# Retention's output products in high and low parts, and 32 pairs of convolution taps multiplied on ScalarE

## The chip, the core and the metric

One Trainium2 chip, one of its cores. The metric is the device time of one execution of the whole program, in microseconds. Engines are named as in the profile: PE is TensorE, with PEld its weight loads, DVE is VectorE, ACT is ScalarE, POOL is GpSimd, SP is SyncE, which issues the loads.

## What is computed

Two blocks over 256 tokens of width 1024, in fp32. The first (gated delta rule, short convolution) is not touched by the change. The second one projects the normalized input into nine pieces and runs two branches over them:

```python
q, k, v, z_ret, u_val, u_gate, z_conv, g_a, g_b = jnp.split(h @ w_in[l], split_at, axis=-1)
# retention: 4 heads, keys of 256, values of 512
scores = einsum('bhid,bhjd->bhij', qc, kc) * decay_mask
inner  = einsum('bhij,bhje->bhie', scores, vc)            # the output products
y_a = (head_groupnorm(o) * silu(z_ret)) @ w_ret_out
# convolution: causal, one filter of 31 taps for each of the 1024 channels
a = u_val * sigmoid(u_gate)
a = causal_depthwise_conv_2(a, conv_w, conv_b)
y_b = (silu(layernorm(a)) * silu(z_conv)) @ w_conv_out
y = (sigmoid(g_a) * y_a + sigmoid(g_b) * y_b) @ w_out
```

The kernel computes the retention without the chunked recurrence: the masked, decayed scores of 256 x 256 tokens times the values.

## The kernel before

**Phases and chunks.** The weights come in chunks of 1 MB, one after the other (`PHASES`, with the number of chunks of each). In the second block the order is glu (8), qk (8), v (8), zret (8), zconv (4), gates (8), ret_out (8), conv_out (4), w_out (4). TensorE goes through the chunks in that order; work that belongs to no chunk stands behind a chunk (`beside`).

**Every product in three.** A weight half chunk (128 x 1024 fp32) is split: ScalarE writes the high part `w_hi` (a copy into the reduced type fp32r, L1220), VectorE the low part `w_lo` = weight minus high part (`part_lo`, L1786). TensorE multiplies high by high, high by low and low by high (in `wide_hi`, L727 and L728, and `wide_lo`, L734, with 512 columns; in `chunk`, L677, L678 and L686, with 256). A wide chunk is 24 products of 128x512. Within a half TensorE waits for `hi_ready` first and for `lo_ready` two thirds on. `w_hi` and `w_lo` have four half slots, so the high part of half h of chunk c can be written when TensorE has done half h of chunk c-2 (`half_done`).

**The step of the other engines.** ScalarE and VectorE run, in program order, one step for each chunk c (`chunks`): first the parts of half 1 of chunk c+1 and of half 0 of chunk c+2, then what the phase gives them (`each`). VectorE's part of it in each phase:

- `rotate` (qk): three operations of the convolution, then the rotation of a 128x512 result out of PSUM (L2445 to L2449).
- `decayed` (v): nine operations of the convolution in steps 0 to 3, eight in 4 to 7, and in steps 0 to 3 the masked scores of a head, `st` (L2459). The values are copied out of PSUM by ScalarE (`tokens_out`, L1641) after every second chunk.
- `group_norm` (zret): seven operations of the convolution, the statistics of one output product (L2477), and in even steps the scalars of the head before (`group_scale`).
- `turned_pairs` (zconv): eight, five, five, five operations, and two low parts of the retention's output, `yT_lo`.
- `last_pairs` (gates): four, then ten in each step until none is left; then the sum over the channels, on which the layer norm of ret_out rests.

**The convolution.** Channels lie in eight groups of 128 partitions, `aP` holds them with 30 zeros in front, `cv` the sums. One operation (`conv_op`, L2396 for tap 0, L2399 for the others) is one tap of one group, 256 wide: `cv = aP[tap:tap+256] * w + cv`. Two groups, a pair, alternate, so that an operation waits on `cv_step` not for the one in front of it but for the one before that. 248 operations in all, in the order pair, tap, group, handed out by `conv_share(n)`.

**The retention.** TensorE computes the scores of head c behind chunk c of v (`scores`, L1134) as fp32 products. Behind chunk c of zret it computes one output product of head c/2 and token block c%2 (`weighted_sums`): one fp32 product of 128x128 by 128x512 for block 0 (L1146), two for block 1 (L1146 and L1148). The profile shows each fp32 product as two instructions. The result lies in one of four PSUM banks. ScalarE normalizes a head's two results in `group_norm` (L1656 square root, L1662), two steps later, and GpSimd multiplies them by the gate (L1773) into `vt`. GpSimd also adds up `cv` of pairs 0 and 1 and then pair 2 (L1777, L1780), when the products by the gate are done and the pair is finished. In zconv TensorE transposes the result (`turn_two`), ScalarE and VectorE write its high and low parts.

**Banks.** In v, zret and gates chunks c and c+1 fill two banks, and chunk c+4 waits until they are read (`bank_free`). Where the reader changes from VectorE to ScalarE or back (`READ_BY`, `HANDED`), the new reader first waits for the old one's last release.

## Time and profile before

| | us |
|---|---|
| three runs | 837.55, 837.8, 839.03 |
| median | 837.8 |
| profiled execution, its own time | 837.87 |
| its span | 836.1 |
| TensorE busy | 827.8 (99%) |
| VectorE busy | 731.1 (87%) |
| ScalarE busy | 500.2 (60%) |
| GpSimd busy | 45.4 (5%) |

The granted TensorE clock is 0.999 of full speed over the span. In the profiled execution the chunks of qk begin at 521.5 us, those of v at 567.6, those of zret at 616.6, of zconv at about 670.8, of gates at 697.2 and of ret_out at about 741. A busy share is the union of an engine's instructions; an instruction can begin before the one in front of it on the same engine has ended, so a duration is longer than the distance between two starts.

### The profile page before, as it was taken

How to read it: one execution, taken by the hardware profiler on the slowest of the kernel's cores; microseconds unless marked ns; L12 is line 12 of the kernel's file. 1: busy time of each engine (PE TensorE's matmuls, PEld its weight loads, DVE VectorE, ACT ScalarE, POOL GpSimd, SP SyncE). 2: the span in 40 equal slices, each digit the busy share in tenths (PEclk: the TensorE clock that was granted, in tenths of full speed). 3: DMA queues.
4: the chain of work that ended last, by engine and by line, in shares of the span. 5: the costliest groups of instructions: out<-in, count | busy, mean ns of one | idle time of the engine just before them, and what ended most of it. 6: DMA issues, size and time to landing. Idle time of an engine off the chain costs nothing.

```text
span 836.1 us, 13942 instructions
## 1 busy us (share of the span) xinstructions
PE 827.8 (99%) x5146; PEld 725.1 (87%) x5146; DVE 731.1 (87%) x1179; ACT 500.2 (60%) x804; POOL 45.4 (5%) x46
## 2 busy tenths in 40 slices
PE   8999999999999999999999999999999999999997
PEld 8999998789888888888888788998887798888886
DVE  7799899868877898888989979999999999988774
ACT  6899858576566555555565775333346675546743
POOL 0001101341100000000000000000001220000000
PEclk9999999999999999999999999999999999999999
DMA  9875675511875877777776656655454435564531
GB/s 277 256 253 169 211 245 174 146 38 45 278 232 179 261 262 263 257 256 252 238 257 218 221 185 213 202 184 169 155 198 151 152 118 200 186 231 171 188 115 50
DMA packets 129882, 164.13 MB, mean 196 GB/s; under 512 B 17407, under 2 KB 92199, under 8 KB 129703
## 3 DMA queue, kind: packets, MB, share of 16 engines
q1 hardware_dynamic: 129831, 163.45, 59.9%
q8 instruction: 33, 0.54, 0.3%
q14 instruction: 18, 0.15, 0.1%
HBM read 159.20 MB, written 4.23 MB: 195 GB/s over the span
## 4 chain that ended last, share of the span: by engine, by line
PE 98%; DVE 1%; DMA 1%; issue 0%; ACT 0%; DVEq 0%; SPq 0%; ACTq 0%
PE psum L695 16%; PE psum L727 14%; PE psum L728 14%; PE psum L734 14%; PE psum L704 8%; PE psum L677 6%; PE psum L686 6%; PE psum L678 6%; PE psum L1028 2%; PE psum L631 1%; PE psum L641 1%; PE psum L635 1%; PE psum L1033 1%; PE psum L915 1%; PE psum L1146 1%; PE psum L1134 1%
## 5 line engine op out<-in xcount | busy, mean ns | idle before, releaser
L1220 ACT ACTIVATE w_hi<-w_raw 128x1024 fp32r<-128x1024 f32 x255 | 266.6, 1061 | 188.2 <-PE psum L734 87.1
L1786 DVE TENSOR_TENSOR w_lo<-w_raw,w_hi 128x1024 fp32r<-128x1024 f32 x256 | 305.2, 1221 | 44.3 <-ACT w_hi L1220 42.2
L695 PE MATMUL psum<-hT,w_hi 128*128 128x512 f32 x576 | 138.9, 391 | 0.0
L695 PEld LDWEIGHTS psum<-hT,w_hi 128*128 128x128 f32 x576 | 105.4, 188 | 20.2
L727 PE MATMUL psum<-w_hi,hT 128*128 128x512 f32 x280 | 113.3, 405 | 0.0
L728 PE MATMUL psum<-w_hi,hT 128*128 128x512 f32 x280 | 109.3, 390 | 0.0
L2399 DVE SCALAR_TENSOR_TENSOR cv<-aP,par,cv 128x256 f32<-128x256 f32 x240 | 107.9, 519 | 0.0
L677 PE MATMUL psum<-hT,w_hi 128*128 128x256 f32 x432 | 107.4, 286 | 0.0
L678 PE MATMUL psum<-hT,w_hi 128*128 128x256 f32 x432 | 105.9, 283 | 0.0
L677 PEld LDWEIGHTS psum<-hT,w_hi 128*128 128x128 f32 x432 | 82.8, 192 | 0.4 <-issue 0.2
L678 PEld LDWEIGHTS psum<-hT,w_hi 128*128 128x128 f32 x432 | 82.9, 192 | 0.3 <-issue 0.2
L704 PEld LDWEIGHTS psum<-hT,w_lo 128*128 128x128 f32 x576 | 74.8, 191 | 3.3
L704 PE MATMUL psum<-hT,w_lo 128*128 128x256 f32 x576 | 76.1, 283 | 0.0
L727 PE MATMUL psum<-w_hi,yT_hi 128*128 128x512 f32 x192 | 75.8, 395 | 0.0
L734 PE MATMUL psum<-w_lo,hT 128*128 128x512 f32 x280 | 75.6, 390 | 0.0
L728 PE MATMUL psum<-w_hi,yT_lo 128*128 128x512 f32 x192 | 74.8, 390 | 0.0
L727 PEld LDWEIGHTS psum<-w_hi,hT 128*128 128x128 f32 x280 | 52.6, 188 | 12.0 <-issue 1.7
L728 PEld LDWEIGHTS psum<-w_hi,hT 128*128 128x128 f32 x280 | 52.6, 188 | 12.0 <-issue 1.7
L734 PEld LDWEIGHTS psum<-w_lo,hT 128*128 128x128 f32 x280 | 52.6, 188 | 11.2
L686 PE MATMUL psum<-hT,w_lo 128*128 128x256 f32 x432 | 60.6, 283 | 0.0
L686 PEld LDWEIGHTS psum<-hT,w_lo 128*128 128x128 f32 x432 | 55.7, 192 | 0.0
L734 PE MATMUL psum<-w_lo,yT_hi 128*128 128x512 f32 x192 | 52.7, 389 | 0.0
(341 smaller groups left out, 1108.6 us busy)
## 6 DMA issues: line engine op xcount, KB each, us to landing
w_raw<-in_w_in_dram SPq DMA_DIRECT2D x44, 1024.0 KB, 5.1
w_raw<-in_sc_w_in_dram SPq DMA_DIRECT2D x32, 1024.0 KB, 7.9
w_raw<-in_gdn_w_in_dram SPq DMA_DIRECT2D x23, 1024.0 KB, 7.1
ada<-in_w_ada_dram SPq DMA_DIRECT2D x24, 512.0 KB, 4.8
w_raw<-in_gdn_w_out_dram SPq DMA_DIRECT2D x8, 1024.0 KB, 5.5
w_raw<-in_sc_w_out_dram SPq DMA_DIRECT2D x8, 1024.0 KB, 6.4
w_raw<-in_w_ret_out_dram SPq DMA_DIRECT2D x8, 1024.0 KB, 5.1
w_raw<-in_w_conv_out_dram SPq DMA_DIRECT2D x4, 1024.0 KB, 5.1
```

The lines of the kernel that those rows point to most:

```text
L677: pe.matmul(o[:, m, :], w_hi[s][:, k, mine], a_hi[:, ka, :], start=m == 0 and ka == 0, stop=False, skip_group_check=True)
L678: pe.matmul(o[:, m, :], w_hi[s][:, k, mine], a_lo[:, ka, :], start=False, stop=False, skip_group_check=True)
L686: mm = pe.matmul(o[:, m, :], w_lo[s][:, k, mine], a_hi[:, ka, :], start=False, stop=ka == KT - 1, skip_group_check=True)
L695: pe.matmul(o, w_hi[s][:, k, mine], hT[:, h * KH2 + k, :, :], start=h == 0 and k == 0, stop=False, skip_group_check=True)
L704: mm = pe.matmul(o, w_lo[s][:, k, mine], hT_hi[:, ka, :], start=False, stop=ka == KT - 1, skip_group_check=True)
L727: pe.matmul(psum[:, b + m, :], a_hi[:, ka, mine], wide(w_hi[s])[:, e, :], start=start and h == 0 and e == 0, stop=False, skip_group_check= ...
L728: pe.matmul(psum[:, b + m, :], a_lo[:, ka, mine], wide(w_hi[s])[:, e, :], start=False, stop=False, skip_group_check=True)
L734: mm = pe.matmul(psum[:, b + m, :], a_hi[:, k + 2 * h + e, mine], wide(w_lo[s])[:, e, :], start=False, stop=stop and h == 1 and e == 1, sk ...
L1028: mm = pe.matmul(b[:, a, :], left(a), right(a), start=True, stop=True)
L1220: act.activation((w_hi[half_slot(g, h)] if home is None else third_hi[half_slot(g, home)])[:, :, :], raw[slot][:, h * KH2:(h + 1) * KH2, : ...
L1786: return dve.tensor_tensor(o, whole, hi.bitcast(F32), ALU.subtract)
L2399: dve.scalar_tensor_tensor(out=cv[:, n, :], in0=src, scalar=w, in1=cv[:, n, :], op0=ALU.mult, op1=ALU.add).then_inc(cv_step, 1)
```

## The change

It has two parts.

*Output products.* The masked scores `st` and the values get high and low parts: ScalarE writes `st_hi` and `vt_hi` (the latter in place of the copy of the values), VectorE `st_lo` and `vt_lo`, in the steps of v. `weighted_sums` multiplies in three, 3 products for block 0 and 6 for block 1 instead of 1 and 2 fp32 ones. The values' banks are now released by VectorE, so the reader changes at zret rather than at v.

*Convolution.* The order of the operations is laid out at build time. 32 (pair, tap) entries are "made": ScalarE multiplies both groups of the pair by their weight (two 256-wide activations) into one of two, later two other, buffers, and VectorE adds the 512-wide buffer to `cv` in one operation. The list `CONV` has 184 single operations and 32 made ones, 216 in all. Per step, singles and made: qk 3 and 0, 3 and 1 in turn; v 6 and 1 four times, 4 and 2 four times; zret 4 and 2 (in step 0: 6 and 2, where a pair ends); zconv 8, 5, 5, 5; gates 4, 10, 10, 10, 7, and none from step 5 on, where the kernel before has 4, five times 10, and 1.

```diff
-READ_BY = {name: "act" if name in ("z", "v", "zret", "zconv", "gates") else "dve" for name in ORDER}
+READ_BY = {name: "act" if name in ("z", "zret", "zconv", "gates") else "dve" for name in ORDER}
+CONV_SHARES = [("glu", [(0, 0), (0, 0), (3, 0), (4, 0), (5, 0), (4, 0), (2, 0), (4, 0)]), ("qk", [(3, 0), (3, 1)] * 4), ("v", [(6, 1)] * 4 + [(4, 2)] * 4),
+               ("zret", [(4, 2)] * 8), ("zconv", [(8, 0), (5, 0), (5, 0), (5, 0)]), ("gates", [(4, 0)] + [(10, 0)] * 7)]
+def tap_before(i):
+    kind, pair, tap, e = CONV[i]
+    return max(j for j in range(i) if CONV[j][1] == pair and (e is None or CONV[j][3] in (None, e))) + 1
...
             def weighted_sums(c):
-                pe.wait_ge(st_ready, min(RH, c + 1))
+                pe.wait_ge(st_ready, RH + h + 1)
...
-                mm = pe.matmul(o, st[:, h, t * P:(t + 1) * P], vt[:, 0, vh], start=True, stop=(t == 0))
-                if t:
-                    mm = pe.matmul(o, st[:, h, SEQ:SEQ + P], vt[:, 1, vh], start=False, stop=True)
+                for b in range(t + 1):
+                    cs = slice(t * P, (t + 1) * P) if b == 0 else slice(SEQ, SEQ + P)
+                    pe.matmul(o, st_hi[:, h, cs], vt_hi[:, b, vh], start=b == 0, stop=False, skip_group_check=True)
+                    pe.matmul(o, st_hi[:, h, cs], vt_lo[:, b, vh], start=False, stop=False, skip_group_check=True)
+                    mm = pe.matmul(o, st_lo[:, h, cs], vt_hi[:, b, vh], start=False, stop=b == t, skip_group_check=True)
...
+            def make_taps(name, c):
...
+                    if k >= 2:
+                        act.wait_ge(cv_step, CONV.index(MADE[k - 2]) + 1)
...
+                        i = act.activation(made_in(k)[:, e, :], aP[:, n, tap:tap + SEQ], ACT.Copy, scale=w)
+                    i.then_inc(tap_made, 1)
...
-            chunks("v", tokens_out(vt, ACT.Copy))
+            def beside_v(i, j, done):
+                c = 4 * i + j
+                make_taps("v", c)
+                if c >= RH:
+                    act.wait_ge(st_ready, RH)
+                    act.wait_ge(sco_done, RH)
+                    act.activation(st_hi[:, c - RH, :], st[:, c - RH, :], ACT.Copy).then_inc(part_hi_ready, 1)
+                if c % 2:
+                    act.wait_ge(half_done, done)
+                    act.activation(vt_hi[:, :, c // 2 * CW2:(c // 2 + 1) * CW2], psum[:, j - 1:j + 1, :], ACT.Copy).then_inc(part_hi_ready, 1)
+            chunks("v", beside_v, unroll=True)
...
             pool.wait_ge(rg_ready, NT * RH)
-            pool.wait_ge(cv_step, CW * 4)
+            pool.wait_ge(cv_step, CONV_ENDS[1])
...
-            pool.wait_ge(cv_step, CW * 6)
+            pool.wait_ge(cv_step, CONV_ENDS[2])
...
+                if tap:
+                    dve.wait_ge(cv_step, tap_before(i))
+                if kind == "made":
+                    k = MADE.index(CONV[i])
+                    dve.wait_ge(tap_made, k + 1)
+                    dve.tensor_tensor(cv[:, both, :], cv[:, both, :], made_in(k)[:, :, :], ALU.add).then_inc(cv_step, 1)
+                    return
...
             def decayed(i, j, done):
                 c = 4 * i + j
-                conv_share(9 if c < RH else 8)
+                conv_share("v", c)
...
+                else:
+                    dve.wait_ge(part_hi_ready, PARTS_BY[c - 1] + 1)
+                    part_lo(st_lo[:, c - RH, :], st[:, c - RH, :], st_hi[:, c - RH, :]).then_inc(st_ready, 1)
+                if c % 2:
+                    dve.wait_ge(part_hi_ready, PARTS_BY[c])
+                    columns = slice(c // 2 * CW2, (c // 2 + 1) * CW2)
+                    part_lo(vt_lo[:, :, columns], psum[:, j - 1:j + 1, :], vt_hi[:, :, columns]).then_inc(bank_free, 2)
```

ScalarE calls `make_taps` in each step of qk, v and zret, behind the high parts of the weights and ahead of the step's other work.

## Rows read from the trace of the kernel before

**Rows 1.** The page: busy time of the engines, and the chain that ended last.

```profile
PE 827.8 (99%) x5146; PEld 725.1 (87%) x5146; DVE 731.1 (87%) x1179; ACT 500.2 (60%) x804; POOL 45.4 (5%) x46
...
PE 98%; DVE 1%; DMA 1%; issue 0%; ACT 0%; DVEq 0%; SPq 0%; ACTq 0%
```

**Rows 2.** Busy us by stage: length, PE, PEld, DVE, ACT, POOL, clock, DMA share, GB/s.

```profile
616.50:670.40 53.90, 53.90 (x219) 40.51 (x217) 51.45 (x92) 34.20 (x36) 8.66 (x6) 1.00 0.49 156
...
697.50:741.00 43.50, 43.50 (x193) 36.02 (x192) 43.50 (x80) 21.46 (x22) 0.00 (x0) 1.00 0.52 171
```

**Rows 3.** VectorE's timeline (start, length, what): zret step 2, zconv steps 0, 1.

```profile
636.12 4.94 DVE L2399 SCALAR_TENSOR_TENSOR cv<-aP,par,cv 128x256 f32<-128x256 f32 x7
...
678.23 6.37 DVE L2399 SCALAR_TENSOR_TENSOR cv<-aP,par,cv 128x256 f32<-128x256 f32 x8
684.51 1.28 DVE L1786 TENSOR_TENSOR yT_lo<-psum,yT_hi 128x512 fp32r<-128x512 f32 x2
685.71 2.35 DVE L1786 TENSOR_TENSOR w_lo<-w_raw,w_hi 128x1024 fp32r<-128x1024 f32 x2
```

**Rows 4.** VectorE's timeline in v, steps 0 and 4.

```profile
576.37 0.55 DVE L2459 TENSOR_TENSOR st<-psum,decay 128x384 f32<-128x384 f32 x1
576.84 1.22 DVE L1786 TENSOR_TENSOR w_lo<-w_raw,w_hi 128x1024 fp32r<-128x1024 f32 x1
...
600.01 3.25 DVE L2399 SCALAR_TENSOR_TENSOR cv<-aP,par,cv 128x256 f32<-128x256 f32 x8
603.17 2.36 DVE L1786 TENSOR_TENSOR w_lo<-w_raw,w_hi 128x1024 fp32r<-128x1024 f32 x2
```

**Rows 5.** TensorE's timeline: low products of zconv's chunk 2, second half.

```profile
688.81 1.12 PE L686 MATMUL psum<-hT,w_lo 128*128 128x256 f32 x8
```

**Rows 6.** TensorE's timeline: two chunk ends in v, then output products of zret.

```profile
610.26 1.07 PE L734 MATMUL psum<-w_lo,hT 128*128 128x512 f32 x4
...
615.70 1.07 PE L734 MATMUL psum<-w_lo,hT 128*128 128x512 f32 x4
...
622.05 1.02 PE L1146 MATMUL psum<-vt,st 128*128 128x512 f32 x2
...
628.40 1.02 PE L1146 MATMUL psum<-vt,st 128*128 128x512 f32 x2
...
635.60 1.02 PE L1146 MATMUL psum<-vt,st 128*128 128x512 f32 x2
```

**Rows 7.** VectorE's timeline in ret_out: four 512-wide operations in a row.

```profile
752.41 2.50 DVE L2526 TENSOR_TENSOR cv<-cv,lnm 128x512 f32<-128x512 f32 x4
```

**Rows 8.** VectorE's timeline in qk: part of a rotation.

```profile
540.85 0.68 DVE L2446 TENSOR_TENSOR rp<-psum,trig 128x512 f32<-128x512 f32 x1
541.57 0.42 DVE L2448 TENSOR_TENSOR qkT<-rp,rp 128x256 f32<-128x256 f32 x1
```

**Rows 9.** VectorE's waits, in v (first row) and zret: us, times, longest.

```profile
DVE w_lo L1786 <- ACT w_hi L1220: 1.8, 4, 0.6
...
DVE w_lo L1786 <- ACT w_hi L1220: 1.7, 3, 1.1
DVE grs L2466 <- ACT grs L1656: 0.4, 1, 0.4
```

**Rows 10.** GpSimd's timeline: the first of four products, and the two sums.

```profile
637.10 2.88 POOL L1773 TENSOR_TENSOR vt<-og,zr 128x512 f32<-128x512 f32 x2 [415.67 <-ACT og L1662]
...
682.16 1.36 POOL L1777 TENSOR_TENSOR ln_sum<-cv 128x512 f32<-128x512 f32 x1
694.84 1.33 POOL L1780 TENSOR_TENSOR ln_sum<-ln_sum,cv 128x512 f32<-128x512 f32 x1 [11.33 <-DVE cv L2399]
```

**Rows 11.** One line's instructions, 636 to 656: ns min/median/max, first and last start.

```profile
L2399 DVE SCALAR_TENSOR_TENSOR cv<-aP,par,cv x21: 472/480/1526, 636.1 to 654.6; 128x256 f32<-128x256 f32 x21
```

**Rows 12.** VectorE's timeline in gates: step 4 begins.

```profile
725.42 2.36 DVE L1786 TENSOR_TENSOR w_lo<-w_raw,w_hi 128x1024 fp32r<-128x1024 f32 x2
```

**Rows 13.** ScalarE's timeline in the first block: six 256-wide ones with a scale.

```profile
67.79 2.49 ACT L1421 ACTIVATE PT<-PT,lnr 128x256 f32<-128x256 f32 x6
```

More of the change, by code:

```diff
@@ L93, with conv_order @@
 SHIFTED = ((4, 5, 6, 7), (6, 7))
+CONV_SHARES = [("glu", [(0, 0), (0, 0), (3, 0), (4, 0), (5, 0), (4, 0), (2, 0), (4, 0)]), ("qk", [(3, 0), (3, 1)] * 4), ("v", [(6, 1)] * 4 + [(4, 2)] * 4),
+               ("zret", [(4, 2)] * 8), ("zconv", [(8, 0), (5, 0), (5, 0), (5, 0)]), ("gates", [(4, 0)] + [(10, 0)] * 7)]
+TAP_PHASES = ("qk", "v", "zret")
+def conv_order():
+    order, ends, part = [], [], {}
+    pair, tap, e = 0, 0, 0
+    for name, counts in CONV_SHARES:
+        for c, (singles, made) in enumerate(counts):
+            mine = part[name, c] = []
+            while (singles or made) and pair < KT // 2:
+                if singles or e or tap == 0:
+                    mine.append(("one", pair, tap, e))
+                    tap, e, singles = tap + e, 1 - e, max(singles - 1, 0)
+                else:
+                    mine.append(("made", pair, tap, None))
+                    tap, made = tap + 1, made - 1
+                order.append(mine[-1])
+                if tap == CW:
+                    ends.append(len(order))
+                    pair, tap = pair + 1, 0
+    assert pair == KT // 2
+    return order, ends, part
+CONV, CONV_ENDS, CONV_PART = conv_order()
+MADE = [entry for entry in CONV if entry[0] == "made"]
+def tap_before(i):
+    kind, pair, tap, e = CONV[i]
+    return max(j for j in range(i) if CONV[j][1] == pair and (e is None or CONV[j][3] in (None, e))) + 1
+PARTS_BY = [sum((d >= RH) + d % 2 for d in range(c + 1)) for c in range(COUNT["v"])]
 E_LEAST = 0.5 * math.log(RMS_EPS) - 0.1
@@ L229, in build @@
         o_t = o_q + 32 * K
+        vt_hi, vt_lo = at("vt_hi", o_q + 16 * K, [P, NT, 2 * D], F32R), at("vt_lo", o_yT + 16 * K, [P, NT, 2 * D], F32R)
         st = at("st", o_t, [P, RH, 3 * P])
+        st_hi, st_lo = (at(n, o_q + 6 * s * K, [P, RH, 3 * P], F32R) for s, n in enumerate(("st_hi", "st_lo")))
         glu, rp1, rp2 = (at(n, o_t + 2 * s * K, [P, 2, SEQ]) for s, n in enumerate(("glu", "rp1", "rp2")))
@@ L1633, in glu_each @@
                 act.activation(glu_part[j % 2][:, :, :], psum[:, 2 * j:2 * j + 2, SEQ:2 * SEQ], ACT.Copy).then_inc(sc_act, 1)
+            def make_taps(name, c):
+                for entry in CONV_PART[name, c]:
+                    kind, pair, tap, _ = entry
+                    if kind != "made":
+                        continue
+                    k = MADE.index(entry)
+                    act.wait_ge(bank_free, 4 + FIRST["qk"])
+                    if k >= 2:
+                        act.wait_ge(cv_step, CONV.index(MADE[k - 2]) + 1)
+                    if made_in(k) is not made[0] and made_in(k) is not made[1]:
+                        act.wait_ge(st_ready, RH)
+                    for e in range(2):
+                        n = 2 * pair + e
+                        w = par[:, 2 + tap // 16, tap % 16 * KT + n:tap % 16 * KT + n + 1]
+                        i = act.activation(made_in(k)[:, e, :], aP[:, n, tap:tap + SEQ], ACT.Copy, scale=w)
+                    i.then_inc(tap_made, 1)
             chunks("glu", glu_each, apart=True)
-            chunks("qk")
+            chunks("qk", lambda i, j, done: make_taps("qk", 4 * i + j), unroll=True)
             def tokens_out(dst, func):
@@ L2397, in conv_op, with conv_share @@
                 else:
-                    dve.wait_ge(cv_step, step - 1)
                     dve.scalar_tensor_tensor(out=cv[:, n, :], in0=src, scalar=w, in1=cv[:, n, :], op0=ALU.mult, op1=ALU.add).then_inc(cv_step, 1)
-            conv_ops = [(pair, tap, e) for pair in range(KT // 2) for tap in range(CW) for e in range(2)]
-            def conv_share(n):
-                for _ in range(min(n, len(conv_ops))):
-                    conv_op(*conv_ops.pop(0))
+            def conv_share(name, c):
+                for entry in CONV_PART[name, c]:
+                    conv_op(conv_done[0])
+                    conv_done[0] += 1
             def glu_each(i, j, done):
```

47 lines of the change are left out of this document (29 added, 18 removed).

## The prediction

> **What bounds the kernel now.** I read the page first: TensorE is busy 99% of the span and the chain of waits that ended last is 98% TensorE [rows 1]. So the time can only fall by taking work off TensorE, and only if nobody makes it wait. The second view is the busy time by stage: in the zret and gates stages VectorE is busy 51.45 of 53.9 and 43.5 of 43.5 us [rows 2]. TensorE never waits there, but VectorE is full. The question for this change is therefore not what VectorE's average is, but how far ahead of TensorE its low parts of the weights (`w_lo`) are, step by step, and what the change does to that lead. That is in the timelines of the two engines.
>
> The code sets the rule. In step c VectorE writes the low part of the second half of chunk c+1 and of the first half of chunk c+2, then does its share of the convolution and the stage's own work. TensorE wants the former in the last third of the second half of chunk c+1. The tightest place for this change is the first low part of zconv's step 1: VectorE starts it at 685.71 [rows 3], two of them take 2.36 and one 1.22, so they begin 1.14 apart [rows 4], so it is done by about 686.85, and TensorE's low products of that half start at 688.81 [rows 5]. The lead there is 1.96 us.
>
> **What TensorE gains.** A chunk of 24 wide products takes 5.44 us (610.26 to 615.70), 0.227 a product [rows 6]. Chunks of zret with an output product take 6.35 and 7.20 us (622.05, 628.40, 635.60) [rows 6], so the products cost 0.91 with one block and 1.76 with two; four of each, 10.68. The change issues 3 and 6 reduced-precision products of the same 128x512 shape: 4 x 9 x 0.227 = 8.16. TensorE gains 2.5 us, if it waits for nothing. That gives 837.87 - 2.5 = 835.3, against the profiled execution's own 837.87.
>
> **What VectorE pays, per operation.** A single tap of the convolution costs 0.397 (eight in 600.01 to 603.17) [rows 4]. A made tap becomes one 512-wide addition. Such additions begin 0.60 apart ((2.50-0.69)/3) [rows 7]. But each made addition waits on `cv_step` for the operation directly in front of it. What that costs is seen in the rotation: `rp2` starts at 540.85, and the next operation, which waits for it, at 541.57: 0.72 instead of 0.60 [rows 8]. I take 0.12 for each such wait. Four singles and two made additions cost 1.59 + 0.72 + 0.72 = 3.03. Eight singles cost 3.16, seven 2.78. So pairs save next to nothing: 0.15 in v, and they add 0.2 in zret. The low parts of the masked scores, 128x384, cost as `st` does, 0.47 (576.37, next at 576.84) [rows 4]; those of the values, 128x1024 out of PSUM, as a weight's low part, 1.14.
>
> The Trainium skill speaks against the 0.12: "VectorE: DVE Perf Modes", section "The DRAIN you can't avoid", says the next operation waits for an empty pipe anyway, so that a semaphore after each costs nothing extra. By that the wait's price would be zero. The trace disagrees (0.72 against 0.60), and the sum goes by the trace.
>
> **VectorE's lag, step by step** (start of a step after the change minus its start now; the loads' and the products' times beside it don't matter while VectorE is behind).
> - qk: four made additions come on top of the same 24 singles, 4 x 0.72 = +2.9, of which some 0.4 fill short waits. v starts 2.5 late, at 573.0. The last rotation ends there too, and TensorE wants it for the first scores when v's chunk 0 is done, 567.6 + 5.44 = 573.0: a wait of 0 to 0.5, which adds nothing in the end, since TensorE waits for VectorE later anyway.
> - v, first four steps: 9 singles (3.57) become 6 singles and a made one (3.10): -1.9. Two low parts of values: +2.3.
> - v, last four: 3.16 becomes 3.0: -0.6. Four `st_lo`: +1.9. Two `vt_lo`: +2.3. In v VectorE waits four times for a high part, 1.8 in all [rows 9]; being late it no longer does: -1.8. Lag 4.4 or so as zret starts (2.5 - 1.9 + 2.3 - 0.6 + 1.9 + 2.3 - 1.8 = 4.7, less some 0.3 in short gaps).
> - zret: step 0 has the end of one pair and the start of the next, 3.7 instead of 2.8: +0.9. The others cost 0.2 more each: +1.4. The waits in it, 1.7 for high parts and 0.4 for ScalarE's root [rows 9], are gone: -2.1. Lag 4.6 as zconv starts. While GpSimd multiplies, seven singles take 4.86 (4.94 less the overlap with the next) [rows 3] instead of 2.78: GpSimd has two operations of 1.4 us there [rows 10], and the longest tap lasts 1526 ns instead of 480 [rows 11]. The wide addition also reads two SBUF tensors, so I keep those 2.1 us per head as they are.
> - zconv, step 0: 6.28 now (678.23 to 684.51) [rows 3], with three GpSimd operations in it (two as in the other heads, and the sum at 682.16). The second sum, now at 694.84 [rows 10], waits for pair 2, which is finished in this step after the change: it moves up into it. Four instead of three collisions, of which the third is only partly felt now, less two cheaper first taps: +0.4. Lag 5.0 at zconv's step 1.
>
> So `w_lo` for the second half of zconv's chunk 2 is ready at 691.85 instead of 686.85, and TensorE, which wanted it at 688.81, gets there 3.0 us later than now: it waits 5.5 us in all (some of it earlier, in zret's chunks 6 and 7 and zconv's 0, 1 and 2) and gives back the 2.5 gained. What is late next: in gates a step with ten taps lasts 3.97 + 2.28 = 6.25 on VectorE, a chunk 5.44, so its lead shrinks by 0.8 a step. In step 4 it starts its first low part at 725.42 [rows 12], done at 726.56; TensorE wants it 4.53 into chunk 5, at 697.2 + 5 x 5.44 + 4.53 = 728.9. The lead there is 2.4, and my lag is 4.2 (5.0, less the 0.8 that GpSimd's second sum no longer costs in zconv's step 2). That asks for 1.8, less than the 3.0 already lost. From step 5 there is nothing left to convolve (41 operations in gates instead of 55, 14 x 0.397 = 5.6 us less), so the mean and all behind it have more room than now. The later stages move by 3.0. Sum: 837.87 + 3.0 = 840.9. The profiled execution stands 0.1 above the median of the runs, 837.8, so 840.8.
>
> **What ScalarE pays.** Six 256-wide activations with a scale per partition out of SBUF take 2.49, 0.40 each [rows 13], so 64 take 25.6. In zret that is 1.6 a step on an engine that is busy 34.2 of 53.9 [rows 2]: 12.8 more makes 47. That fits, but its order matters: a made pair waits until VectorE has used up the buffer of two pairs ago, and behind it on ScalarE stand the group norm, the copy of `zr` and the next high parts. VectorE takes up those high parts later still (it is 4 to 5 us behind), which is the cover; I cost it at nothing. At the start of zret ScalarE also waits for VectorE's last `vt_lo` (about 623.9), with high parts behind it that TensorE needs from about 629 on (zret's chunk 2): nothing. Cover gone, by an activation at 0.7 instead of 0.4, it would be the rival below. No DMA is moved; the ring of weights is freed by VectorE's low parts, up to 5 us later than now, four chunks (22 us) ahead: nothing.
>
> **Rivals.**
> 1. *VectorE keeps its lead* and the 2.5 us arrive: 835.3, faster. It needs a lag at zconv's step 1 below 1.96 - 2.5, that is 0.5 less than today, so 5.5 less than my sum. For it: the change removes 64 singles (25.4) for 32 wide additions (19.2), which is the other half of what is added. Against: 32 gaps of 0.12, four `st_lo` and four `vt_lo` (6.4), all placed ahead of the tight step, while the taps saved are taken from the end of gates. It decides if GpSimd's collisions vanish. 0.12.
> 2. *Made additions are cheaper than I think*: the wait on the operation in front costs nothing, or GpSimd doesn't hold up the wide addition, or it takes 0.52. Some 45 such waits lie ahead of the tight step, so the first would take 5 us off VectorE's work, but VectorE that has caught up waits for high parts again, as it does now [rows 9], and the four collisions in zconv's step 0 stay; each alone leaves a lag of about 2 to 2.5 there: 837.9 to 838.4, no change. For it: no row has the exact operation. Against: the gap and the 0.60 are rows of the same shape. 0.24. The rule of the Trainium skill given above would make it this rival's first kind.
> 3. *ScalarE becomes the bound*: at 0.7 an activation, the pair takes 1.4, the group norm and the high parts behind it come late, and TensorE waits for high parts from zret's chunk 4 on, 4.4 us more: 845. Against it stands the row at 0.40. 0.06.
>
> **How the numbers follow.** My forecast has 0.58, with its own range of 839.0 to 843.0: a gap of 0.15 instead of 0.12 gives +1.4 (45 of them), an addition at 0.66 instead of 0.60 gives +1.9 (32), a `vt_lo` at half its price -1.8 (four, less what turns into waiting). Over 0.2% (1.7 us, about what measuring this kernel can tell) is above 839.5. Slower: 0.53 of the forecast's 0.58, and rival 3: 0.59. Same: rival 2 and the forecast's lower edge: 0.28. Faster: 0.13. The range reaches down to 836.3, which takes in rival 2 and leaves out rival 1, and up to 844.2, where the two dearer prices come together (840.8 + 1.4 + 1.9); it leaves out rival 3.
>
> **What would show it.** In the changed profile: the two kinds of output product 0.68 and 1.36 beyond a 5.44 chunk; TensorE waits for `w_lo` of VectorE in late zret and zconv, some 5 us in all, none after; zret's first low part near 623.8 and zconv's step 1 near 690.7; made additions 0.72 apart; ScalarE's pairs 0.8. If VectorE's step 1 of zconv starts before 687, or made additions run 0.60 apart, I am wrong.

## The result and the profile after

| | before | after |
|---|---|---|
| median of the runs, us | 837.67 (six runs) | 841.5 (six runs, 840.69 to 843.0) |
| ratio, 95% interval | | 1.0047 (1.0035 to 1.0059) |
| profiled execution, its own time | 837.87 | 841.28 |
| its span | 836.1 | 839.5 |

The change makes the kernel 3.8 us slower; 3.0 were forecast. The page of the kernel after, busy time and the chain that ended last, where [rows 1] had 98% TensorE:

```profile
PE 827.0 (99%) x5158; PEld 727.3 (87%) x5158; DVE 733.0 (87%) x1155; ACT 527.2 (63%) x872; POOL 45.2 (5%) x46
...
PE 77%; DVE 20%; issue 2%; DMA 1%; ACT 0%; DVEq 0%; SPq 0%; ACTq 0%
```

The busy shares hardly move. The chain does: a fifth of it is now VectorE, so somewhere VectorE lets TensorE wait. TensorE's waits from qk to ret_out (what it waited for, us in total, times, longest) say for what:

```profile
PE psum L731 <- DVE w_lo L1861: 2.9, 2, 1.9
PE psum L779 <- DVE w_lo L1861: 0.8, 1, 0.8
PE psum L1207 <- ACT og L1736: 0.6, 1, 0.6
PE psum L722 <- ACT w_hi L1267: 0.2, 1, 0.2
```

And TensorE's timeline (start, length, what, in brackets the wait before it) says where, zret's chunk 6 and zconv's chunks 0 and 2 (the third line is the transposes behind zconv's chunk 1):

```profile
660.68 1.19 PE L779 MATMUL psum<-w_lo,hT 128*128 128x512 f32 x4 [0.78 <-DVE w_lo L1861]
...
675.18 1.22 PE L731 MATMUL psum<-hT,w_lo 128*128 128x256 f32 x8 [0.99 <-DVE w_lo L1861]
...
683.60 1.30 PE L1207 MATMUL psum<-const,vt 128*128 128x128 f32 x8 [0.57 <-ACT og L1736]
...
692.12 1.22 PE L731 MATMUL psum<-hT,w_lo 128*128 128x256 f32 x8 [1.95 <-DVE w_lo L1861]
```

The last line answers [rows 5]: the same products, at 688.81 before, now at 692.12.

**Positions.** The waits named above sum to 4.5 us. What is lost is more, 6.2 (below). Some 0.6 of the difference lies in groups that last longer behind a wait (1.22 instead of 1.12, 1.19 instead of 1.07, the transposes 1.30 instead of 1.03); where the other 1.1 lie is not shown. The safe reading is TensorE's position: the start of the same low products in two kernels. One thing has to be taken off. Executions enter qk up to 2.2 us apart, whatever the change (low products around qk's start at 517.79 before, 517.46 after), so every difference below is a start minus the start in the kernel before, minus the same difference at that point. For the kernel after at zconv's chunk 2: 692.12 - 688.81 + 0.33 = +3.64. All the runs, in us:

| kernel | enters qk | zret chunk 6, first half | zconv chunk 2, second half | gates chunk 0 | ret_out |
|---|---|---|---|---|---|
| before (starts) | 517.79 | 659.07 | 688.81 | 699.12 | 742.63 |
| after | -0.33 | -1.73 | +3.64 | +3.73 | +3.74 |
| after, second profile | +0.74 | -1.70 | +3.67 | +5.35 | +5.37 |
| products alone | +0.87 | -1.89 | +0.45 | +0.53 | +1.67 |
| taps alone | +0.53 | +0.20 | +2.18 | +3.86 | +3.87 |
| balanced, 12 pairs | +0.14 | -1.89 | -2.49 | -2.51 | -2.50 |
| balanced, no pairs | +0.10 | -1.81 | -2.42 | -2.43 | -2.42 |
| before, new shares | +1.67 | 0.0 | 0.0 | 0.0 | 0.0 |
| after, late GpSimd sum | +1.02 | -1.71 | +2.66 | +2.75 | +2.76 |
| after, three activations a pair | +0.80 | -1.12 | +7.95 | +9.59 | +9.60 |
| products, 24 pairs in place | -0.56 | -1.90 | -0.16 | -0.08 | +0.68 |
| before, 3 taps earlier | +0.18 | 0.0 | 0.0 | 0.0 | 0.0 |
| before, 8 taps earlier | +1.61 | 0.0 | +1.49 | +1.60 | +1.61 |
| before, 13 taps earlier | +0.39 | 0.0 | +4.15 | +5.84 | +5.86 |

In the row "after" TensorE first gains on the kernel before (the output products), then loses it and 3.7 more in zconv, and from there to the end keeps its distance: gates and what follows add nothing.

VectorE's timeline in zconv's steps 0 and 1, which answers [rows 3] (678.23, 684.51 and 685.71 before):

```profile
682.55 0.88 DVE L2484 SCALAR_TENSOR_TENSOR cv<-aP,par,cv 128x256 f32<-128x256 f32 x2
683.35 1.69 DVE L2482 TENSOR_SCALAR cv<-aP,par 128x256 f32<-128x256 f32 x2
684.96 4.78 DVE L2484 SCALAR_TENSOR_TENSOR cv<-aP,par,cv 128x256 f32<-128x256 f32 x4
689.65 1.28 DVE L1861 TENSOR_TENSOR yT_lo<-psum,yT_hi 128x512 fp32r<-128x512 f32 x2
690.85 2.35 DVE L1861 TENSOR_TENSOR w_lo<-w_raw,w_hi 128x1024 fp32r<-128x1024 f32 x2
```

The low part that TensorE wants for 692.12 starts at 690.85. What stands beside the slow four taps is GpSimd, in its timeline; its second sum, at 694.84 in [rows 10], is now the last line here:

```profile
683.53 2.65 POOL L1848 TENSOR_TENSOR vt<-og,zr 128x512 f32<-128x512 f32 x2 [11.61 <-ACT og L1736]
686.26 1.36 POOL L1852 TENSOR_TENSOR ln_sum<-cv 128x512 f32<-128x512 f32 x1
687.70 1.35 POOL L1855 TENSOR_TENSOR ln_sum<-ln_sum,cv 128x512 f32<-128x512 f32 x1
```

### The profile page after: what moved, and what is told of

Its sections match the earlier page's. It is cut to its first block, busy times and chain, and to the rows that moved or that the text cites. A ratio compares the mean times of both kernels' runs of the same rounds, so it can differ in the third digit from the quotient of the medians.

```text
span 839.5 us, 14042 instructions
## 1 busy us (share of the span) xinstructions
PE 827.0 (99%) x5158; PEld 727.3 (87%) x5158; DVE 733.0 (87%) x1155; ACT 527.2 (63%) x872; POOL 45.2 (5%) x46
## 4 chain that ended last, share of the span: by engine, by line
PE 77%; DVE 20%; issue 2%; DMA 1%; ACT 0%; DVEq 0%; SPq 0%; ACTq 0%
PE psum L740 15%; PE psum L772 10%; PE psum L773 10%; PE psum L779 10%; PE psum L749 8%; DVE w_lo L1861 7%; DVE cv L2484 5%; PE psum L731 4%; PE psum L722 4%; PE psum L723 4%; PE psum L1073 2%; DVE cv L2476 2%; PE psum L676 1%; PE psum L686 1%; PE psum L680 1%
## 5 line engine op out<-in xcount | busy, mean ns | idle before, releaser
L772 PE MATMUL psum<-w_hi,hT 128*128 128x512 f32 x280 | 110.4, 394 | 0.0
L773 PE MATMUL psum<-w_hi,hT 128*128 128x512 f32 x280 | 109.2, 390 | 0.0
L2484 DVE SCALAR_TENSOR_TENSOR cv<-aP,par,cv 128x256 f32<-128x256 f32 x176 | 79.2, 511 | 0.0
```

The costliest lines, as they stand in the source:

```text
L772: pe.matmul(psum[:, b + m, :], a_hi[:, ka, mine], wide(w_hi[s])[:, e, :], start=start and h == 0 and e == 0, stop=False, skip_group_check= ...
L773: pe.matmul(psum[:, b + m, :], a_lo[:, ka, mine], wide(w_hi[s])[:, e, :], start=False, stop=False, skip_group_check=True)
L2484: dve.scalar_tensor_tensor(out=cv[:, n, :], in0=src, scalar=w, in1=cv[:, n, :], op0=ALU.mult, op1=ALU.add).then_inc(cv_step, 1)
```

## The experiments

The theory: in the kernel before, VectorE is 1.96 us ahead of TensorE at zconv's step 1, and what the change puts in front of that point beyond the lead comes out as a wait. The rivals: the made taps are the loss by their own cost (waits, GpSimd), or ScalarE's added work is, or the parts of scores and values are and can't be helped.

### Each half of the change alone

The products alone, with the old shares of the convolution:

```diff
-CONV_SHARES = [... ("qk", [(3, 0), (3, 1)] * 4), ("v", [(6, 1)] * 4 + [(4, 2)] * 4), ("zret", [(4, 2)] * 8), ...
+CONV_SHARES = [... ("qk", [(3, 0)] * 8), ("v", [(9, 0)] * 4 + [(8, 0)] * 4), ("zret", [(7, 0)] * 8), ...
```

> Retention's products in high and low parts, the convolution as it was: every tap on VectorE, its additions shared out over the chunks as before. Theory (VectorE is 2.0 us ahead of TensorE at zconv step 1 in the kernel before, and what is added to it beyond that comes out as TensorE waits): the two part_lo kinds add about 4.6 us to VectorE between qk and zret, the products give TensorE 2.5 us back, so the sum is a TensorE that stands 1.1 us later than before at the start of ret_out, 838.9 us where before is 837.7, with waits of about 3.6 us in zret and zconv. Rival A (the made taps are the whole loss, the parts fit into the lead): 835.2 us. Rival B (the loss is ScalarE's: its copies and pairs delay the high parts of the activations): without pairs ScalarE is lighter by 28 us, and the time is 835.2 us too, but with waits of TensorE for w_hi in the run with the pairs and not for w_lo.

Measured: 839.85 us, ratio 1.0017 (1.0008 to 1.0026), which is 1.4 us over the kernel before (1.7 by the medians). TensorE's waits for low parts over the whole span:

```profile
PE psum L731 <- DVE w_lo L1861: 1.3, 2, 1.1
...
PE psum L779 <- DVE w_lo L1861: 0.5, 1, 0.5
```

By position 1.67 are lost, 0.53 of them up to gates. The other 1.1 appear in gates' chunks 6 and 7, where 55 operations leave VectorE no room [rows 2, 12]. The expectation had all of it in zret and zconv: the place was partly missed, the size short by 0.6. Both rivals that gave 835.2 are out: with these shares the parts of scores and values do not fit into the lead.

The taps alone: `weighted_sums`, the copy of the values and `decayed` as before, `make_taps` and the new shares kept.

```diff
...
+            v_tokens = tokens_out(vt, ACT.Copy)
             def beside_v(i, j, done):
-                c = 4 * i + j
-                make_taps("v", c)
-                if c >= RH:
-                    ...
+                make_taps("v", 4 * i + j)
+                v_tokens(i, j, done)
...
```

> The 32 pairs of tap products on ScalarE and their 512-wide additions on VectorE, with Retention's output products in fp32 as they were (scores and v in one part, v copied out by ScalarE). Theory: TensorE gets nothing back; the wait of a made addition for the one in front (0.12 us) and GpSimd's holding of VectorE cost the lead of 2.0 us and a little over, 839.2 us, with a first wait of about 1.3 us at zconv chunk 2. Rival A (a made tap costs VectorE less than the pair it replaces, so this half of the change alone is a gain or nothing): 837.7 us, no wait. Rival B (ScalarE's pairs are the loss): 841 us or more, with waits for w_hi.

Measured: 840.76 us, ratio 1.0031 (1.0022 to 1.0039), 2.6 over the kernel before. By position 2.18 at zconv's chunk 2, 0.7 more than the 1.5 expected (839.2 less 837.7); the 1.68 that come behind it are the clock's (below). So this half, which gives TensorE nothing, costs by itself with these shares, and it isn't "a gain or nothing". Rival B expected waits of TensorE for `w_hi`, and there are none. But ScalarE is not out of it: its pairs stand in front of the square root of the group norm, and in zret VectorE waits 2.0 us for that root, where it waits 0.4 in the kernel before [rows 9]:

```profile
638.17 0.17 DVE L2543 RECIPROCAL grs<-grs 128x2 f32<-128x2 f32 x1 [1.99 <-ACT grs L1723]
```

How much of the 2.18 this is, no run shows; the whole change has no such wait, because its VectorE comes later. The halves must not be added up either. At zconv's chunk 2 they have 0.45 and 2.18 and the whole has 3.64, more than both, since each half alone may use up the lead and the whole can use it only once. At ret_out 1.67 and 2.18 come near the whole's 3.74 by chance: 1.1 of the 1.67 are lost in gates, where the whole loses nothing.

### Another sharing of the same work

```diff
-("qk", [(3, 0), (3, 1)] * 4), ("v", [(6, 1)] * 4 + [(4, 2)] * 4), ("zret", [(4, 2)] * 8), ("zconv", [(8, 0), (5, 0), (5, 0), (5, 0)]), ("gates", [(4, 0)] + [(10, 0)] * 7)
+("qk", [(3, 0)] * 8), ("v", [(8, 0)] * 4 + [(5, 1)] * 4), ("zret", [(2, 1), (8, 1)] * 4), ("zconv", [(5, 0)] * 4), ("gates", [(4, 0)] + [(9, 0)] * 7)
```

> The kernel after with the same kinds of work shared out differently: 12 pairs made by ScalarE in place of 32, 5 to 8 taps in v's chunks, 2 taps and 1 pair in zret's even chunks (where GpSimd holds VectorE up) against 8 and 1 in the odd ones, 5 in each zconv chunk, 9 in the chunks of gates (which have room at their end). Theory: no step of VectorE ends later than TensorE needs it, the products' gain of 2.5 us is whole: 835.2 us, and no TensorE wait for w_lo between qk and ret_out. Rival A (what hurts is the parts themselves, in v and at zret's start, and can't be moved away by shares): 838 to 841 us. Rival B (ScalarE): 20 pairs fewer are 16 to 18 us less on ScalarE, and the time falls in proportion, about 839 us.

Measured: 835.66 us, ratio 0.9973 (0.9964 to 0.9982): 2.3 to 2.5 us faster than the kernel before, and 2.50 by position. The page and TensorE's timeline (to set beside 692.12 above):

```profile
PE 98%; DVE 1%; DMA 1%; issue 0%; ACT 0%; DVEq 0%; SPq 0%; ACTq 0%
...
686.46 1.12 PE L731 MATMUL psum<-hT,w_lo 128*128 128x256 f32 x8
```

VectorE's step 1 of zconv starts at 682.93, ahead of the kernel before, though step 0 still has GpSimd beside it:

```profile
677.51 4.14 DVE L2484 SCALAR_TENSOR_TENSOR cv<-aP,par,cv 128x256 f32<-128x256 f32 x5
...
682.93 2.36 DVE L1861 TENSOR_TENSOR w_lo<-w_raw,w_hi 128x1024 fp32r<-128x1024 f32 x2
```

The parts of scores and values are all there, so they are no fixed price. But 20 pairs fewer are in it too. The next run takes out the rest of them, with shares of their own:

```diff
+("qk", [(3, 0)] * 8), ("v", [(9, 0)] * 8), ("zret", [(4, 0), (8, 0)] * 4), ("zconv", [(5, 0)] + [(4, 0)] * 3), ("gates", [(9, 0)] + [(8, 0)] * 7)
```

> Retention's products in high and low parts, no pair made by ScalarE, and the convolution's taps shared out anew: 3 single taps in each chunk of qk as before, 9 in each of v, 4 and 8 in zret's even and odd ones (before: 7 and 7), 5 and then 4 in zconv (before: 8 and then 5), 9 and then 8 in gates (before: 4 and then 10). Theory (what counts is that no step of VectorE ends later than TensorE needs it; a made tap saves VectorE about 0.1 us or less, and the room of gates is enough without it): the whole 2.5 us of the products, 835.2 us, and no TensorE wait for w_lo. Rival A (the pairs are needed for the gain, since 12 of them were in the balanced kernel): 837.5 to 838.9 us. Between them stands a wait at the end of gates or at the mean, where VectorE's last taps run later than before: 836 to 837 us.

Measured: 836.07 us, ratio 0.9973 (0.9964 to 0.9982; 1.7 us faster by the medians, 2.3 by the ratio), position -2.42. ScalarE's pairs are not needed for any of the gain. Are the shares alone? The kernel before with these shares:

```diff
-                conv_share(9 if c < RH else 8)
+                conv_share(9)
...
-                conv_share(7)
+                conv_share(8 if n % 2 else 4)
...
-                conv_share(5 if j else 8)
+                conv_share(4 if j else 5)
...
-                conv_share(10 if c else 4)
+                conv_share(8 if c else 9)
```

> The kernel before, with nothing changed but the shares of the convolution, which are those of the run without pairs (9 in each chunk of v, 4 and 8 in zret, 5 and then 4 in zconv, 9 and then 8 in gates). Theory: TensorE waits for nothing there in the kernel before, so a better sharing has nothing to give back: 837.7 us (no change). Rival: the gain of the balanced kernels comes from the shares and not from the products: 835.2 us.

Measured: 838.09 us, ratio 0.9999 (0.999 to 1.0008). No: the gain is the products', and the shares only let it through.

### What the pairs themselves do

```diff
-("qk", [(3, 0), (3, 1)] * 4), ("v", [(6, 1)] * 4 + [(4, 2)] * 4), ("zret", [(4, 2)] * 8)
+("qk", [(3, 0), (1, 1)] * 4), ("v", [(9, 0), (5, 2)] * 2 + [(4, 2)] * 4), ("zret", [(7, 0), (3, 2)] * 4)
```

> The kernel after with every tap back in the chunk in which the kernel before computes it, but 24 of them still made as pairs by ScalarE and added 512 wide (a pair in place of two singles: 3 and 1+1 in qk's chunks, 9 and 5+2 and then 4+2 in v's, 7 and 3+2 in zret's). Against the run with the products alone it differs by these pairs only. Theory (a made addition is 0.72 us where two single taps are 0.80 us, so 24 pairs save VectorE at most 2 us, of which 16 or so lie before the first wait; what cost the kernel after 2 us more than the products alone is that 12 more half taps were taken into the chunks up to zconv): 838.3 to 838.8 us, 0.4 us below the products alone up to their 1.4 us over the kernel before. Rival A (the pairs cost: waits for ScalarE, or made additions held up more by GpSimd): 841 us, as the kernel after. Rival B (each pair saves 0.2 us, since an addition has less to do): 836 us.

Measured: 838.31 us, ratio 1.0006 (0.9997 to 1.0015); position -0.16 at zconv's chunk 2 and +0.68 at ret_out, where the products alone have +0.45 and +1.67. So 24 pairs save TensorE 1.0 us, 0.04 each, once they replace taps where these were. That leaves the shares. Before, 171 operations lie in qk to zconv and 55 in gates. After, it is 185 (a made one counted as two) and 41; in this run 173, since a pair can't be split at a step's end. The 12 between this run and the kernel after are 12 times 0.397, 4.8 us of VectorE, moved from gates, where VectorE then has nothing to convolve in steps 5 to 7, to a place in front of the tight step. The kernel after stands 3.8 later at that step (+3.64 and -0.16), with 8 pairs more to its credit; where the rest of the 4.8 went is not shown.

### The lead

The kernel before, with the share of zconv's chunk 0 raised, which moves taps from gates in front of VectorE's step 1:

```diff
-                conv_share(5 if j else 8)
+                conv_share(5 if j else 11)
```

> The kernel before with the convolution's share of zconv chunk 0 raised from 8 taps to 11; the last chunks of gates get the less. It puts 3 taps of 0.40 us, 1.2 us, in front of VectorE's low part for TensorE's products of zconv chunk 2. Theory (VectorE is 1.96 us ahead there): no TensorE wait, 837.7 us. Rival (the lead is not what decides, and VectorE's work comes out at once): 838.9 us.

Measured: 837.83 us, ratio 0.9998 (0.9989 to 1.0007), no wait. With 16 instead of 11:

> The same with 16 taps in zconv chunk 0, 3.2 us more than in the kernel before, and the GpSimd sum that waits for the third pair of rows comes one chunk earlier. Theory (lead 1.96 us; what is over it comes out as a wait at zconv chunk 2): a wait of 1.2 to 1.7 us and 839.2 us. Rival A (no lead: everything shows): 840.9 us. Rival B (waits there are made good later, since gates has room): 837.7 us. And if the granted clock falls after such a wait, as it did after the 1.84 and 1.95 us waits of other runs, 1.7 us come on top in the profiled run.

Measured: 839.89 us, ratio 1.0019 (1.001 to 1.0028), position +1.60. VectorE and TensorE:

```profile
679.82 9.53 DVE L2399 SCALAR_TENSOR_TENSOR cv<-aP,par,cv 128x256 f32<-128x256 f32 x16
...
690.47 2.52 DVE L1786 TENSOR_TENSOR w_lo<-w_raw,w_hi 128x1024 fp32r<-128x1024 f32 x2
```

```profile
PE psum L686 <- DVE w_lo L1786: 1.4, 1, 1.4
```

Step 1 starts at 690.47, that is 3.15 later than before (685.71 plus the 1.61 of the entry): 8 taps of 0.397. Less the lead of 1.96 it is 1.2; the low part is also slower, 2.52 for two, with GpSimd's sum beside it. 1.2 us of VectorE cost nothing and 3.2 cost 1.6. That is the lead, measured without the change.

The lead can be read more closely, as the lag of VectorE's step 1 (its start in a kernel less 685.71, less the entry) less TensorE's position at zconv's chunk 2. In the kernel after it is 5.47 - 3.64 = 1.83, in its second profile 5.51 - 3.67, for the products alone 2.29 - 0.45, for the taps alone 4.02 - 2.18, for the 24 pairs in place 1.68 + 0.16, for the late sum below 4.49 - 2.66, for three activations a pair 9.79 - 7.95, for 13 taps earlier 5.99 - 4.15: 1.83 or 1.84 each time. With 3 taps earlier the lag is 1.18 and nothing is lost. So one number of VectorE, its lag at this step, gives TensorE's loss there in every kernel of this case that waits there, but for the one above, where GpSimd's sum lies on the low part itself and it is 1.66. It is a little under the 1.96 worked out before, since TensorE's products begin 1.27 behind the start of the low part (690.85, 692.12) and not 1.14.

### GpSimd's second sum

```diff
-            pool.wait_ge(cv_step, CONV_ENDS[2])
+            pool.wait_ge(cv_step, CONV.index(CONV_PART["zconv", 3][-1]) + 1)
```

> The kernel after with one wait changed: GpSimd's second sum of the convolved pairs is made after the convolution's share of zconv chunk 3, not beside that of chunk 0. Theory: VectorE's second and fourth taps of zconv step 0 are no longer held up by it, TensorE's wait at zconv chunk 2 falls from 1.95 to about 1.0 us, and the time from 841.5 to 840.6 us. Rival A (the sum holds nothing up that matters, since the collision is only moved to gates): 841.5 us. Rival B (the collision costs more in gates): 842 us or more.

The medians don't settle it (841.26 us, ratio 1.0038, 1.0025 to 1.005). The profile does: position +2.75 at gates against +3.73, and in VectorE's timeline of zconv's step 0 the four taps, 4.78 above, take 3.75:

```profile
683.95 0.88 DVE L2484 SCALAR_TENSOR_TENSOR cv<-aP,par,cv 128x256 f32<-128x256 f32 x2
...
686.35 3.75 DVE L2484 SCALAR_TENSOR_TENSOR cv<-aP,par,cv 128x256 f32<-128x256 f32 x4
690.02 1.28 DVE L1861 TENSOR_TENSOR yT_lo<-psum,yT_hi 128x512 fp32r<-128x512 f32 x2
```

The sum held them up by 1.03 us, in one collision, and 0.98 of it reached TensorE (+3.64 and +2.66 at zconv's chunk 2).

### ScalarE

```diff
+                        if e:
+                            act.activation(made_in(k)[:, e, :], aP[:, n, tap:tap + SEQ], ACT.Copy, scale=w).then_inc(tap_made, 1)
+                            act.wait_ge(tap_made, 2 * k + 1)
                         i = act.activation(made_in(k)[:, e, :], aP[:, n, tap:tap + SEQ], ACT.Copy, scale=w)
...
-                    dve.wait_ge(tap_made, k + 1)
+                    dve.wait_ge(tap_made, 2 * k + 2)
```

> The kernel after, with the second activation of every made pair done twice (the repeat waits for the first), which adds 32 activations of 0.4 to 0.5 us and their waits to ScalarE, 16 of them in zret, and nothing to VectorE. Theory (ScalarE in zret has about 9 us of room in 53, taken in lumps, so most of the 1 us a chunk is swallowed): 843.6 us, the 2.1 us over the kernel after as longer waits in zret's chunk 6 and zconv's chunk 0. Rival A (ScalarE sets the pace of the kernel after already): all of zret's 8 to 10 us show, 849 us or more. Rival B (ScalarE never matters): 841.5 us.

Measured: 847.08 us, ratio 1.0099 (1.0084 to 1.0114), 4.2 us over the kernel after on the same chip, twice the expected. What carries them is a wait that the kernel after doesn't have, VectorE's for the square root of the group norm, which stands behind the made taps on ScalarE (the total, and the last of the three):

```profile
DVE grs L2560 <- ACT grs L1733: 4.0, 3, 1.5
```

```profile
673.21 0.17 DVE L2560 RECIPROCAL grs<-grs 128x2 f32<-128x2 f32 x1 [1.52 <-ACT grs L1733]
...
696.30 2.34 DVE L1864 TENSOR_TENSOR w_lo<-w_raw,w_hi 128x1024 fp32r<-128x1024 f32 x2
```

Two clock drops are in its profile, in zret (behind a wait of 2.47) and in zconv (behind 1.95), of 1.6 us each. Only the second shows in the time. The first reaches neither VectorE nor ScalarE: VectorE's three waits for the root end at 640.95, 657.08 and 673.21, 16.13 apart both before the drop (which begins near 665) and across it, and TensorE waits for VectorE behind it anyway. At zconv's chunk 2 the position is VectorE's lag less the lead, 9.79 less 1.84, that is 7.95, against 3.67 in the kernel after: 4.3 us, all of them ScalarE's, against 2.1 expected.

The added activations from v to zconv, by line (busy time, mean ns of one, idle before):

```profile
L1696 ACT ACTIVATE made<-aP,par 128x256 f32<-128x256 f32 x27 | 13.4, 495 | 0.0
```

32 activations of 0.5 us more cost 4.2. The 64 that the change adds were not the bound, but there was next to no room behind them. In the kernel after ScalarE has the root of the second head at 653.04, and VectorE takes it at 653.27:

```profile
652.75 0.29 ACT L1730 ACTIVATE grs<-gmv,eps_n 128x2 f32<-128x2 f32 x1
```

```profile
653.27 0.15 DVE L2557 RECIPROCAL grs<-grs 128x2 f32<-128x2 f32 x1
```

That is 0.2 us of room; for the heads before and behind it is 0.3.

### The clock behind a wait

The kernel after once more, beside the others:

> The kernel after, unchanged, beside the others on one chip: 841.5 us, 3.8 us over the kernel before. The theory expects the TensorE waits at the same four places (zret chunk 6, zconv chunks 0, 1 and 2), 5.5 to 6 us together against the 2.5 us given back, whatever the position at which TensorE enters qk.

Measured: 842.86 us, ratio 1.0053 (1.0039 to 1.0067). The positions are those of the first profile to 0.03 us up to zconv's chunk 2, and the wait there is the same 1.95. Behind it they part. Stretches 688 to 692, 692 to 694, 694 to 697, 697 to 700 (busy time of PE, PEld, DVE, ACT, POOL, then the granted clock), first of the first profile, then of the second:

```profile
688.00:692.00 4.00, 2.17 (x16) 1.97 (x16) 4.00 (x6) 4.00 (x6) 1.06 (x1) 1.00 0.00 0
692.00:694.00 2.00, 1.88 (x17) 1.89 (x17) 2.00 (x5) 0.87 (x3) 0.00 (x0) 1.00 0.32 48
694.00:697.00 3.00, 3.00 (x27) 3.00 (x26) 3.00 (x6) 1.89 (x3) 0.00 (x0) 1.00 0.84 317
```

```profile
688.00:692.00 4.00, 3.04 (x24) 2.63 (x22) 4.00 (x6) 4.00 (x7) 2.08 (x2) 1.00 0.00 0
692.00:694.00 2.00, 0.78 (x6) 0.78 (x7) 2.00 (x3) 1.34 (x2) 0.00 (x0) 1.00 0.00 0
694.00:697.00 3.00, 3.00 (x17) 3.00 (x16) 3.00 (x8) 1.81 (x4) 0.00 (x0) 0.51 0.83 260
697.00:700.00 3.00, 3.00 (x25) 3.00 (x25) 3.00 (x4) 1.06 (x2) 0.00 (x0) 0.92 0.31 100
```

In the second the clock is granted at 0.51, the lower of its two levels (1.2 instead of 2.4 GHz), for some 3 us, and the position goes from +3.67 to +5.35. Is it the idle time? The kernel before with one long wait at the same place, 21 taps in zconv's chunk 0:

> The kernel before with 21 taps in zconv chunk 0 where it has 8, so that VectorE comes some 4 us too late for TensorE's products of zconv chunk 2, in the same place where the wait of 1.95 us of the kernel after lies. Theory of the lead: a wait of 4.1 us and 841.9 us. Two views of the granted clock, which in one profiled run of the kernel after stayed at 1.00 behind its 1.95 us wait and in another fell to 0.75 for 5 us: if what makes it fall is the idle time of TensorE there, it falls here in every run, by 1.7 us, and the time is 843.6 us with no second group of times; if it is something else in that kernel (its waits in zret, one after the other), it stays at 1.00 here.

Measured: 844.67 us, ratio 1.0081 (1.0067 to 1.0095), all five runs between 844.1 and 845.4, 1.1 over the 843.6 of the view in which the clock falls every time; the profiled one is the shortest, 844.12. The wait is 4.0, and the clock falls:

```profile
PE psum L686 <- DVE w_lo L1786: 4.0, 1, 4.0
```

```profile
694.00:696.00 2.00, 2.00 (x11) 2.00 (x11) 2.00 (x6) 0.55 (x1) 0.00 (x0) 0.50 0.65 144
696.00:698.00 2.00, 2.00 (x16) 2.00 (x15) 2.00 (x5) 1.58 (x4) 0.00 (x0) 0.80 0.97 377
```

The position goes from +4.15 to +5.84: 1.69 for the clock on top of the wait, with nothing of the change in the kernel. That a shorter wait does it only in part of the executions can be seen in the taps alone, whose wait is 1.84: four executions with a mean clock of 0.997 took 842.27, 842.24, 842.0 and 840.94 us, the seven with 0.999 or 1.0 took 839.4 to 841.1. What decides between them no run shows.

## Why the prediction was right, and where it was off

- **TensorE's gain, 2.5.** Right: -2.50 by position wherever VectorE leaves it alone. The output products of the kernel after begin 0.227 apart, and chunks last 6.12 and 6.80 (628.00 less 621.88, 634.80 less 628.00), 0.68 and 1.36 over 5.44:

```profile
621.88 0.39 PE L1193 MATMUL psum<-vt_hi,st_hi 128*128 128x512 f32 x1
622.11 0.39 PE L1194 MATMUL psum<-vt_lo,st_hi 128*128 128x512 f32 x1
...
628.00 0.39 PE L1193 MATMUL psum<-vt_hi,st_hi 128*128 128x512 f32 x1
...
634.80 0.39 PE L1193 MATMUL psum<-vt_hi,st_hi 128*128 128x512 f32 x1
```

- **A made addition 0.72.** Right: the timeline of VectorE in qk has three single taps, begun at 533.14, then a made one 1.31 later, 0.12 more than three times 0.397, and the rotation, which doesn't wait for it, 0.61 behind. Two made ones in a row, at zret's start, begin 0.73 apart (1.42 less 0.69):

```profile
533.14 1.27 DVE L2484 SCALAR_TENSOR_TENSOR cv<-aP,par,cv 128x256 f32<-128x256 f32 x3
534.45 0.69 DVE L2476 TENSOR_TENSOR cv<-cv,made 128x512 f32<-128x512 f32 x1
535.06 0.68 DVE L2529 TENSOR_TENSOR rp<-psum,trig 128x512 f32<-128x512 f32 x1
...
620.70 1.42 DVE L2476 TENSOR_TENSOR cv<-cv,made 128x512 f32<-128x512 f32 x2
```

  By the rule of the Trainium skill ("VectorE: DVE Perf Modes", "The DRAIN you can't avoid") they would begin as far apart as independent ones, 0.60; the trace disagrees again.
- **GpSimd holds up the wide additions too.** Right. A zret step with GpSimd beside it, of four taps and two made additions, takes 5.06 (639.03 to 644.09) instead of 3.03, 2.0 more, where I kept the 2.1 of the single taps:

```profile
639.03 2.71 DVE L2484 SCALAR_TENSOR_TENSOR cv<-aP,par,cv 128x256 f32<-128x256 f32 x4
641.77 2.40 DVE L2476 TENSOR_TENSOR cv<-cv,made 128x512 f32<-128x512 f32 x2
644.09 0.69 DVE L2568 BATCH_NORM_STATS2 gst<-psum 128x6 f32<-128x512 f32 x1
```

- **VectorE's lag.** v +2.5, zret +4.4, zconv +4.6, its step 1 +5.0 were forecast; 572.80, 623.64, 680.04 and 690.85 less the starts before, plus 0.33, are +2.65, +4.48, +4.66 and +5.47. The first three are right to 0.15. The last is the term that was mis-sized: zconv's step 0, for which I put +0.4, got +0.82 (682.55 to 689.65, 7.10 instead of 6.28). Without GpSimd's second sum the step takes 6.07 (683.95 to 690.02 in the run above), 0.2 less than before, so my +0.4 had 0.6 for a collision that costs 1.03. The agreement in zret is in part luck. By my own prices a step there is 0.25 longer (3.03 less 2.78), so seven are +1.7 and not the +1.4 of the sum (and v's last four -0.5 and not -0.6), which would have made the lag 5.4 and the forecast 841.3. Measured, a step is 6.11 instead of 5.84, and what made up for it is that VectorE got back some 2.4 us of waits and gaps there, and not 2.1.
- **From the lag to the time.** 3.0 was forecast at zconv's chunk 2 and 3.74 is lost: 0.47 is the lag, 0.13 that TensorE begins 1.27 and not 1.14 behind the start of the low part, and 0.1 the stretched group (3.64 there, 3.73 at gates).
- **The waits.** 5.5 in all, in zret's chunks 6 and 7 and zconv's 0, 1 and 2; they are 3.74 + 2.50 = 6.2, and zret's chunk 7 has none. A first 0.16 is at v's first scores, where I had 0 to 0.5. The sum of the profile's wait lines, 4.5, would have confirmed "some 5 us" for the wrong reason: it leaves out 1.7 us that are lost by position.
- **Gates adds nothing.** Right for this kernel (+3.73 and +3.74). With the old shares it would have been wrong: the products alone lose 1.1 there. The 14 operations taken out of gates are the likely reason that it was true; the 24 pairs in place, with all but two of the operations left in gates, lose 0.8 there.
- **ScalarE at nothing.** Right for the time, and the price of an activation too: four in a row last 1.71 and one 0.50, so they begin 0.40 apart. But it was right by luck. I looked at VectorE's use of the high parts for cover and not at the root of the group norm, which has 0.2 to 0.3 us of room; 0.5 us a pair more cost 4.2. Rival 3, which I gave 0.06, was nearer than that, and by another path than the one I described: VectorE waits for the root, and TensorE for VectorE.
- **What was not in the sum.** The granted clock. A change that makes TensorE wait 1.95 us in one place can pay 1.7 more in part of its executions. It explains the second measurement of the kernel after, 5.1 us over the kernel before. It does not explain why the first has 3.8 and not 3.0: its profile has no drop and stands at 3.74.
- **Rivals and range.** The full gain (1) was named with its condition, a lag below -0.54 at zconv's step 1; the balanced kernel meets it (682.93 less 685.71, less 0.14: -2.92) and has the gain. Cheaper made additions (2) and a ScalarE bound (3) did not happen. The range's upper edge, 840.8 + 1.4 + 1.9, is 844.1, not 844.2; it makes no difference.

What I did not ask is whether the loss was the change's or its schedule's. I saw that the work was added ahead of the tight step "while the taps saved are taken from the end of gates", and used it as an argument for a loss, but read it as a fact about the change. The runs show that it was the cause, and that the work can be placed otherwise.

## What to carry to other kernels

When one engine is the bound and another is full beside it, look at the lead of the full one step by step: work put in front of its tightest step costs all that is over the lead, while the same work behind it costs nothing as long as the steps there keep a lead of their own (the products alone lost 1.1 us in gates), and so a change can lose 3.8 us in one sharing and gain 2.5 in another. Place added work by that lead, away from the steps where a third engine holds the full one up, before judging whether the work is worth it. Ask the same of the engine that looks idle: ScalarE was busy 63% and had 0.2 us of room at one point. And compare kernels by the position of the same instruction, corrected for where the stretch begins, rather than by the sum of the wait lines.

## What the runs showed of the hardware

- **A wait can cost TensorE its clock.** Behind waits of 1.84 (taps alone), 1.95 (second profile of the kernel after), 2.47 and 1.95 (three activations a pair) and 4.0 us the granted clock fell to about half for some 3 us, which cost TensorE 1.6 to 1.7; behind the 1.95 of the first profile and waits of 1.4 and less it did not. The same kernel with the same wait did both.
- **GpSimd against VectorE.** Four 128x256 taps out of SBUF take 4.78 us with the end of GpSimd's products and two of its sums beside them, 3.75 with the end of the products and one sum, and 1.6 alone: a sum of 1.35 us takes 1.0 from VectorE. The Trainium skill ("SBUF — State Buffer", in its list of terms) says of the port pair that the two engines share that the loser blocks fully for the other's whole instruction; the trace agrees in kind, with 1.0 of 1.35.
- **Activations with a scale per partition**, 128x256 out of SBUF, begin 0.40 apart in [rows 13] and in the made pairs, and 0.53 apart where one waits for the one in front of it (653.05 and 653.58, with three activations a pair).
